# Diagonal convolution-weight matrices of a hybrid decoder layer: built on chip by ScalarE and GpSimd in place of a load from DRAM

## The reference

```python
h = _rmsnorm(x, g_mix)
proj = h @ w_in                       # 1024 -> 10240: q,k,v,g | GLU input (2x1024) | q_xa | 3 gates
...
def _conformer_conv(glu_in, conv_buf, conv_w, conv_b, ln_g, ln_b, w_conv_out):
    a, gt = jnp.split(glu_in, 2, axis=-1)
    u = a * jax.nn.sigmoid(gt)
    ext = jnp.concatenate([conv_buf.astype(u.dtype), u], axis=1)
    y = lax.conv_general_dilated(ext, conv_w[:, None, :].astype(u.dtype), (1,), 'VALID',
                                 dimension_numbers=('NWC', 'WIO', 'NWC'),
                                 feature_group_count=D_CONV) + conv_b      # width 31, depthwise
    y = _standardize(y) * ln_g + ln_b
    y = jax.nn.silu(y) @ w_conv_out
    return y, ext[:, -(CONV_WIDTH - 1):]
...
merged = gates[:, :, 0] * ret_out + gates[:, :, 1] * conv_out + gates[:, :, 2] * xa_out
x = x + merged @ w_out
x = x + jnp.square(jax.nn.relu(_rmsnorm(x, g_ffn) @ w_up)) @ w_down
```

## Time and profile before

| | us |
|---|---|
| median of 2 runs | 2463.33 (2455.59 to 2471.06) |
| the profiled execution, slowest core | 2466.5 |
| its span in the profile (core 4) | 2465.0 |
| spans of the 8 cores | 2429.8 to 2465.0 |

### The profile page before, as it was taken

The page is one execution under the profiler, slowest core; times in us unless marked ns, Lnnn a source line. Parts: engine busy times, 40 slices in busy tenths (PEclk is TensorE's granted clock), DMA queues, the critical chain, the costliest instruction groups (busy, mean ns, idle before and its releaser), DMA issues.

```text
span 2465.0 us, 29879 instructions; the slowest of 8 cores (2429.8 to 2465.0 us)
## 1 busy us (share of the span) xinstructions
PE 1874.3 (76%) x9605; PEld 926.8 (38%) x9605; DVE 693.0 (28%) x1447; ACT 753.1 (31%) x1254; POOL 351.9 (14%) x377
## 2 busy tenths in 40 slices
PE   4385888876886988999599899959988944535565
PEld 2133333433343334444344344433434422324343
DVE  1224103321423033333402332350134123333202
ACT  1114215321143153323414432251344123434222
POOL 1142003100230021006001200510030001100120
PEclk9697999988998999999799999989999975555667
DMA  8599699999631242554034335513533458779766
GB/s 156 139 189 192 148 192 224 203 194 216 217 137 36 100 152 103 180 188 170 17 107 148 116 131 187 171 69 117 190 119 113 154 192 261 231 265 313 240 225 244
DMA packets 132292, 415.81 MB, mean 169 GB/s; under 512 B 9006, under 2 KB 79022, under 8 KB 105900
## 3 DMA queue, kind: packets, MB, share of 16 engines
q1 hardware_dynamic: 66732, 321.99, 37.4%
q0 software_dynamic: 63104, 83.53, 20.3%
q10 hardware_dynamic: 2304, 8.39, 1.1%
HBM read 389.40 MB, written 80.73 MB: 191 GB/s over the span
## 4 chain that ended last, share of the span: by engine, by line
PE 55%; DMA 23%; DVE 7%; ACT 7%; issue 5%; POOL 1%; SPq 0%; DVEq 0%; ACTq 0%; POOLq 0%
PE ps L421 54%; ACT arena L406 6%; DMA arena<-cv 3%; DMA arena<-w_dn 3%; DMA arena<-sret 3%; DMA arena<-w_up 3%; DVE arena L412 2%; DVE arena L409 2%; DMA arena<-scr_w 2%; DMA arena<-w_in 2%; PE ps L424 2%; DMA srs<-arena 1%; DMA arena<-xp 1%; DMA scr_w<-arena 1%; DVE arena L684 1%
## 5 line engine op out<-in xcount | busy, mean ns | idle before, releaser
L421 PE MATMUL ps<-arena 128*128 128x512 bf16 (+8 forms) x8756 | 1787.0, 366 | 415.6 <-ACT arena L406 152.0
L421 PEld LDWEIGHTS ps<-arena 128*128 128x128 bf16 (+2 forms) x8756 | 845.8, 108 | 1340.6 <-issue 619.9
L406 ACT ACTIVATE arena<-arena 128x1 f32<-128x1 f32 (+11 forms) x548 | 365.8, 686 | 653.9 <-DVE arena L409 132.6
L409 DVE TENSOR_TENSOR arena<-ps,arena 128x512 f32<-128x512 f32 (+5 forms) x438 | 245.1, 590 | 957.7 <-ACT arena L406 587.1
L406 ACT ACTIVATE arena<-ps 128x512 f32<-128x512 f32 (+4 forms) x464 | 252.4, 556 | 734.4 <-PE ps L421 714.1
L409 POOL TENSOR_TENSOR arena<-arena 128x512 f32<-128x512 f32 (+5 forms) x242 | 258.7, 1082 | 864.1 <-DVE arena L827 444.2
L412 DVE SCALAR_TENSOR_TENSOR arena<-ps,arena 128x256 f32<-128x256 f32 (+3 forms) x301 | 160.7, 546 | 282.3 <-ACT arena L406 264.3
L424 PE MATMUL ps<-arena 128*128 128x128 bf16 (+3 forms) x848 | 106.5, 280 | 151.4 <-ACT arena L406 144.7
L424 PEld LDWEIGHTS ps<-arena 128*128 128x128 bf16 (+3 forms) x848 | 85.1, 135 | 173.5 <-issue 169.7
L406 ACT ACTIVATE arena<-ps,arena 128x256 bf16<-128x256 bf16 (+3 forms) x108 | 54.6, 521 | 245.4 <-PE ps L421 242.5
L412 DVE SCALAR_TENSOR_TENSOR arena<-arena,ps 128x512 f32<-128x512 f32 x128 | 85.6, 685 | 101.7 <-PE ps L421 96.0
(11 more groups left out here) (49 smaller groups left out, 157.1 us busy)
## 6 DMA issues: line engine op xcount, KB each, us to landing
arena<-scr_w SPq DMA_DIRECT2D x164, 1024.0 KB, 5.8
scr_w<-arena SPq DMA_DIRECT2D x40, 1024.0 KB, 9.9
arena<-scr_dg SPq DMA_DIRECT2D x32, 992.0 KB, 5.0
arena<-w_in POOLq DMA_DIRECT2D x20, 1024.0 KB, 19.3
arena<-sret SPq DMA_DIRECT2D x16, 1024.0 KB, 10.4
srs<-arena POOLq DMA_DIRECT2D x16, 1024.0 KB, 7.5
arena<-ck SPq DMA_DIRECT2D x32, 512.0 KB, 5.6
arena<-cv SPq DMA_DIRECT2D x32, 512.0 KB, 5.9
```

Source lines behind the costliest of these rows:

```text
L406: S.op("act", lambda e: e.activation(out, in_, func, **kw), r, w)
L409: S.op(eng, lambda e: e.tensor_tensor(out, a, b, op), r, w)
L421: S.op("pe", lambda e: e.matmul(out, lhsT, rhs, start=start, stop=stop), r, w)
```

## The change

The host tensor `dgw` is gone; in its place comes `cwcol` [128, 8x31] with the taps of each channel, loaded once at the start into a constant tile `cwt` on the SyncE queue. `DG.get` is called with a key and a `builder`. The first time for a key the builder is run in place of the load: 31 operations that each write one 128x128 matrix of the buffer as identity times a per-partition scalar, the 16 even taps as a Copy with a scale on ScalarE, the 15 odd taps as a tensor-scalar multiply on GpSimd. Each of the 31 names the same written token, `(self.tok, slot)`, and reads none. The bf16 store to scratch follows as before, and later calls load the scratch as before. `look` of `DG` becomes 0: operations stand where `get` is called. The calls move: in the prompt `get(0)` stands behind glu_stage(0), and `get(cc+1)` behind glu_stage(cc+1) and ahead of conv_stage(cc); in the decode pass `get(0)` stands ahead of the loop over j, behind the loads of `sconv`, and `get(cc+1)` just ahead of the convolution of cc.

```diff
@@
-    dgw = din("dgw", [8, 128, CW, 128])
+    cwcol = din("cwcol", [128, 8 * CW])
...
+    cwt = A.tile([8, CW], F32)
...
+    S.dma("sp", lambda e: e.dma_start(out=cwt, in_=cwcol.rearrange("p (a b) -> p a b", a=8)), w=["c_cw"])
...
-        def get(self, src, key=None):
+        def get(self, src, key=None, builder=None):
             i = self.i
             self.i += 1
             slot = i % self.n
             dst = self.views[slot]
             store = None
+            if builder is not None and key not in self.scr:
+                builder(dst, (self.tok, slot))
+                sap = nc.dram_tensor("scr_%s_%d" % (self.tok, len(self.scr)), [128] + list(self.shape), BF16,
+                                     kind="Internal").ap()
+                self.scr[key] = sap
+                self.anchors.append(S.marker())
+                S.dma("sp", lambda e: e.dma_start(out=sap, in_=dst), r=[(self.tok, slot)], w=[("scr", self.tok, key)])
+                return slot
...
-            if i >= self.look:
+            if self.look > 0 and i >= self.look:
...
+    def diag_builder(cc):
+        def build(dst, tok):
+            for jt in range(CW):
+                if jt % 2 == 0:
+                    ACT(dst[:, jt, :], ident_b, AF.Copy, [], [tok], scale=cwt[:, cc, jt:jt + 1])
+                else:
+                    TS("pool", dst[:, jt, :], ident_b, cwt[:, cc, jt:jt + 1], None, ALU.mult, None, [], [tok])
+        return build
+
     W = WStream(wbuf, "w", 2, [8, 512])
-    DG = WStream(dgbuf, "dg", 1, [CW, 128])
+    DG = WStream(dgbuf, "dg", 0, [CW, 128])
...
-        def conv_stage(cc):
-            ds_ = DG.get(dgw[cc], ('dg', cc))
+        def conv_stage(cc, ds_):
...
         glu_stage(0)
+        dsl = {0: DG.get(None, ('dg', 0), diag_builder(0))}
         for cc in range(8):
             if cc + 1 < 8:
                 glu_stage(cc + 1)
-            conv_stage(cc)
+                dsl[cc + 1] = DG.get(None, ('dg', cc + 1), diag_builder(cc + 1))
+            conv_stage(cc, dsl[cc])
...
+        dsn = [DG.get(None, ('dg', 0), diag_builder(0))]
         for j in range(2):
...
-                ds_ = DG.get(dgw[cc], ('dg', cc))
+                ds_ = dsn[0]
+                if cc + 1 < 8:
+                    dsn[0] = DG.get(None, ('dg', cc + 1), diag_builder(cc + 1))
```

More of the change, by code:

```diff
@@ L346, in build @@
     S.op("dve", lambda e: e.memset(ones_f, 1.0), w=["c_ones"])
-    CONST = ["c_identf", "c_identb", "c_cv", "c_rowb", "c_mask", "c_masks", "c_css", "c_ones", "c_sel"]
+    CONST = ["c_identf", "c_identb", "c_cv", "c_cw", "c_rowb", "c_mask", "c_masks", "c_css", "c_ones", "c_sel"]
     NSLOT = 4
@@ L1417, in host_consts @@
     cw = np.asarray(inp["conv_w"][0], f32)
[L1418 to L1422, removed]
+    c["cwcol"] = np.ascontiguousarray(cw.reshape(CW, 8, 128).transpose(2, 1, 0).reshape(128, 8 * CW))
     return c
```

## The result

The changed kernel is slower: 2580.19 us median against 2461.05, ratio 1.048 with a 95% interval of 1.0458 to 1.0502. The profiled execution took 2581.0 us (span 2579.4, on core 2), 114.5 more than the one before. Forecast were 2560 us (ratio 1.039) and a range of 2515 to 2630.

The account below looks back on a forecast made before the run. TensorE was taken to bound the kernel, the change counting only in tile 0's convolution. Builds net of the stall +81.7, clock +14, constant load 0.5: +96 us on the 2463.3 median, about 2560 us; range 2515 to 2630.

Parts of the forecast that it names:

- part 2: Tile 0's convolution: 31 build operations share one token, handed between ScalarE and GpSimd 30 times; 1.09 us a pair, 16.7 a build.
- B: Time to build one group's 31 matrices in tile 0: 15 pairs and one Copy, 16.7 us, bounds 12.5 to 24.2.
- part 3: Tile 0's ScalarE queue: next build precedes the Identity, alternating with 7.0 us to Sigmoid's end; period 13.05 to 23.7, +82 us.
- part 4: Tile 0's convolution: TensorE idles about 11 us a period, then runs slower; 2.0 us seven times, +14 us (9 to 39).
- parts 1 and 5: Removed reads save only tile 0's 7.0 us stall; moved calls cost 0, at most 3 in decode; constant load 0.5.
- Slower on GpSimd: Rival, tile 0's build: GpSimd multiply takes 0.9 us, build 24.2, +156 us, 2620 us; chance 0.14.
- The clock stays low through the stage: Rival, tile 0's convolution: TensorE stays at its lower clock level, +39 in place of +14, 2585 us; chance 0.13.
- The build hides: Rival, tile 0: engines overlap or build falls under 6.5 us; period stays 13.05, stall goes, 2455 us; chance 0.05.
- Slower by less than 2%: Rival, tile 0's convolution: a build takes between 6.5 and 10.7 us, about 2490 us; chance 0.06.

## Why the prediction was right, and where its sizes were off

- *Only tile 0's convolution counts, and the load was worth 7 us there.* Right in the main. In the mean of the cores the stage took 114.7 of the 127.8 us. TensorE's wait for the load was 7.0 us on the core that was read, but 7.0 to 11.7 on the 8 cores, and with the slow clock behind it 10.7 us in the mean. Building without the chain won back 9 us (cores 0 to 3 of the run with a token for each matrix) and 11 us of stage.
- *Even and odd taps are one chain through two engines (part 2).* Right, by the timeline and by the per-matrix tokens. The size was low: B is 19.4 us, not 16.7, and GpSimd's busy time rose by 66 us, not 40. The term that was mis-sized is the GpSimd tensor-scalar, taken as 0.40 us "near the two-input row" and measured as 0.60; it is above the two-input operation's interpolated 0.45, so the argument that one operand less should put it under that failed, and the price lay inside the stated bounds (0.18 to 0.9). The Copy (0.40 against 0.39) and the hand-overs (0.17 and 0.10 against 0.20 and 0.10) were near. The multiply adds 15 x 0.20 = 3.0 us to a build, the shorter hand-over takes 0.4 back; 8 x 2.6 = 21 us of the total, about what the forecast was low by. (The low bound of B adds up to 12.6 by its own terms, not 12.5, and 49 us are reached at B = 10.8, not 10.7; nothing hangs on either.)
- *The Trainium skill's "roughly line-rate" for one input* (GPSIMD Engine Reference, Engine selection): the estimate of 0.29 us that was worked out from it disagrees with this trace, 0.60 in the chain and 8.71 / 15 = 0.58 back to back. The measurement decides. Only one size was measured, so whether the rate or the fixed cost of the instruction is off can't be told; nor was it tried whether the scalar operand or the bf16 type makes the difference.
- *The build takes turns with 7 us of other work (part 3).* Right: with the clock kept up the period was 26.45 = 19.4 + 7.05, and off ScalarE the same or a longer build cost less.
- *The clock, +14 us (part 4).* Right: six periods of 28.34 in the mean less 19.36 and 7.0 leave 2.0 each, and Identity(6) to Identity(7) took 12.5 in place of 9.6, together 15 us. The granted clock of 0.67 behind the wait and the run with 62 matmuls (1.9 us a period) agree. The wait itself was 14.0 us, not 11, since the build was longer. The sum with the measured B: 8 x 19.36 - 52.2 + 14.8 = 117.5 (B and the clock term now come from the same periods, so this says that nothing else is in them), and the profiled stages differ by 223.96 - 106.42 = 117.5 us (from the table load at the head of the stage, 250.62 and 258.45, to Identity(7), 474.58 and 364.87).
- *The moves and the rest of tile 0 (parts 1 and 5).* The moves cost nothing. That the freed reads give nothing back held as well: behind the stage nothing became shorter, in the mean it was 7.5 us longer. That was not forecast; the prediction had named a change of another stage's length as a sign of being wrong. The first 47.7 us behind Identity(7) are the same on all cores. TensorE's waits for the two `w_co` loads behind them grew from 7.7 to 13.3 us in the mean, and the loads took 22.6 us to land in place of 19.2. Why stays open. The run that filled the waits with 62 matmuls has 3.4 of the 7.5 us, the others at most 1.8; and the profiled execution of the changed kernel was 8.6 us above the mean of 10 executions in its mean core span (2573.7 and 2565.1), so this may belong to that one execution.
- *The rivals.* "Slower on GpSimd" was half true (0.60, not 0.9). "The clock stays low through the stage" is out: the level is back at 1.00 for the convolution of each period that was looked at. "The build hides" needs the per-matrix tokens or VectorE, and then it comes out as that rival said, within 2%. "Slower by less than 2%" would have needed a B under 10.7; it was 19.4.

## What to carry to other kernels

The token or tag by which a scheduler orders writes decides whether two engines share work or hand it to each other: give each independently written part its own. Before work is put on an engine that looks idle, read what its in-order queue does next for the engine that bounds the stage; here the Copies kept ScalarE busy for 6.4 of the 19.4 us of a build, but an Identity of 0.7 us stood behind them and waited for it all. Saved traffic is worth only the wait that the chain shows for it; read that wait on every core (7.0 to 11.7 us here), not on one.

## What the runs showed that was not expected

- A GpSimd multiply of a 128x128 bf16 matrix by a per-partition scalar takes 0.60 us (0.58 back to back), more than the 0.45 interpolated for the two-input float32 operation.
- A wait of an operation for the one before it on its own engine costs too: GpSimd 0.77 us a matrix against 0.58, VectorE 0.36 against 0.17, ScalarE 0.49 against 0.30 (16 Copies in 4.77 us), though a single Copy shows as 0.40.
- The length of a wait alone does not tell what clock follows. Behind waits of 2.6 and 3.2 us TensorE was granted 0.80 (266.8 to 275.0, token for each matrix, core 1) and 0.65 (325.2 to 333.6, 50 matmuls), behind 0.93 us 1.00; but in the run on VectorE the last convolution took 6.86 us at 1.00 behind a wait of 3.5 us, ahead of which stood only the 1.96 us of the ones matmuls and a wait of 0.93 us.
